# A third raw buffer and a second DMA queue for the second expert table of a decoder step on one Trainium2 core

## The reference, cut to what matters

```python
def one_block(xb):                 # 128 tokens at a time
    ...                            # scores of product keys, top 16 of 8 heads: eidx, gate
    u = u_tab[eidx]
    act = gelu(einsum('thkd,td->thk', u, xb))
    return einsum('thk,thkd->td', gate * act, v_tab[eidx])
out = x + peer; y = rmsnorm(out, w_norm_final)
```

## Time and profile before

| what | us |
|---|---|
| median of 3 runs (lowest, highest) | 3672.82 (3670.59, 3683.72) |
| the profiled execution's own time | 3685.51 |
| its span | 3683.6 |
| PE busy in the span | 3517.7 (95%) |
| DVE busy | 2571.1 (70%) |
| ACT busy | 1314.7 (36%) |
| POOL busy | 924.7 (25%) |

### The profile page before, as it was taken

How to read it: one execution, slowest core, us unless ns; L and a number is a source line. 1 busy time by engine, 2 the same in 40 slices (tenths; PEclk the granted TensorE clock), 3 DMA queues, 4 the chain that set the end, 5 groups by cost and what they waited for, 6 DMA issues and landing times. The chain is left out here.

```text
span 3683.6 us, 46625 instructions
## 1 busy us (share of the span) xinstructions
PE 3517.7 (95%) x17879; PEld 3071.5 (83%) x17879; DVE 2571.1 (70%) x3799; ACT 1314.7 (36%) x1675; POOL 924.7 (25%) x619
## 2 busy tenths in 40 slices
PE   8999999998989999999999999998999999999997
PEld 6877777776867889999999999997778787787885
DVE  4135545553233249999998888885888898898897
ACT  5111134442233223332237667762222232232223
POOL 0000000000000000233333333331444454454453
PEclk9999999999989999999999999999999999999998
DMA  5145343435334244788789999998889899899996
GB/s 204 48 147 168 112 135 128 144 110 184 139 122 146 86 176 152 274 320 340 294 323 360 381 384 379 380 384 338 349 334 363 337 347 364 338 348 363 356 356 264
DMA packets 193646, 964.86 MB, mean 262 GB/s; under 512 B 19697, under 2 KB 67121, under 8 KB 92706
## 3 DMA queue, kind: packets, MB, share of 16 engines
q1 hardware_dynamic: 121010, 516.50, 38.1%
q0 software_dynamic: 61424, 426.27, 29.8%
q10 hardware_dynamic: 11008, 19.26, 1.5%
HBM read 865.58 MB, written 96.37 MB: 261 GB/s over the span
## 5 line engine op out<-in xcount | busy, mean ns | idle before, releaser
L2068 PE MATMUL hidden_hp<-dense_hi,whi 128*128 128x384 f32 x2048 | 699.0, 341 | 6.1 <-PEq L123 6.1
L1836 ACT CAST whi<-raw 128x2048 fp32r<-128x2048 f32 x214 | 410.7, 1919 | 818.1 <-PE outputs_vp L2623 512.7
L2069 PE MATMUL hidden_hp<-dense_lo,whi 128*128 128x384 f32 x2048 | 690.8, 337 | 0.0
L2621 PE MATMUL outputs_vp<-whi,outputs_w_hi 128*128 128x512 f32 x1536 | 606.6, 395 | 51.4 <-DVE wlo L1840 38.3
L2015 POOL DMA_INDIRECT hidden_row<-u_rows,expert_ids x192 | 366.0, 1906 | 999.8 <-DVE dots L2300 621.9
L2622 PE MATMUL outputs_vp<-whi,outputs_w_lo 128*128 128x512 f32 x1536 | 603.8, 393 | 0.0
L2623 PE MATMUL outputs_vp<-wlo,outputs_w_hi 128*128 128x512 f32 x1536 | 603.1, 393 | 0.0
L1840 DVE TENSOR_TENSOR wlo<-raw,whi 128x2048 fp32r<-128x2048 f32 x214 | 490.0, 2290 | 111.0 <-ACT whi L1836 107.2
L2355 POOL DMA_INDIRECT outputs_row<-v_rows,outputs_id x192 | 373.0, 1943 | 561.0 <-DVE accg L2547 522.2
L2547 DVE SCALAR_TENSOR_TENSOR accg<-outputs_row,outputs_w_op,accg 128x2048 f32<-128x2048 f32 x192 | 451.3, 2351 | 88.5 <-DMA outputs_row<-v_rows,outputs_id 76.6
L2300 DVE CUSTOM_DVE_ANT_0 hidden_row<-hidden_row,hidden_h_row 128x2048 f32<-128x2048 f32 x192 | 436.8, 2292 | 66.9 <-DMA hidden_row<-u_rows,expert_ids 65.9
(11 more groups left out here) (384 smaller groups left out, 4901.0 us busy)
## 6 DMA issues: line engine op xcount, KB each, us to landing
raw<-v_units SPq DMA_DIRECT2D x128, 1024.0 KB
raw<-u_units SPq DMA_DIRECT2D x86, 1024.0 KB
raw<-w_in SPq DMA_DIRECT2D x42, 1024.0 KB, 5.5
hidden_raw<-u_units SPq DMA_DIRECT2D x42, 1024.0 KB
hidden<-hidden_hid SPq DMA_DIRECT2D x128, 192.0 KB
gate_mat<-units_big SPq DMA_DIRECT2D x12, 2048.0 KB, 20.2
units_big<-hidden SPq DMA_DIRECT2D x16, 1536.0 KB, 13.2
units_big<-gate_mat SPq DMA_DIRECT2D x16, 1536.0 KB, 18.9
```

Of the source, the lines that this page charges most:

```text
L1836: self.nc.scalar.copy(self.hi[s][:], self.raw[raw][:]).then_inc(self.hi_done, 1)
L2068: mm(o, un.hi[s][:, x, :], h_hi[:, x, :], start=x == 0, stop=False)
L2069: mm(o, un.hi[s][:, x, :], h_lo[:, x, :], start=False, stop=False)
L2621: mm(o[:], W_hi[s][:, e, at], hi[x][:, k, :], start=e == 0, stop=False)
```

## The change

Five edits, all for the stage `outputs`:

1. A third raw buffer (`deepen`), so the load of unit n+3 waits for the low part of unit n. SP then issues only the loads of the units.
2. The five loads of `sums` (the residual, 4.5 MB) at the stage's start go from SP's queue to ACT's, and SP's first DMA is the load of unit 2. Their semaphore is split in three, for the prompt rows, the sample rows and the dense tiles.
3. The two halves of a chunk's weights are issued by ACT, the hidden activations after the split of unit 0, the gates after that of unit 1. The DVE and ACT work on them moves one unit later: `weigh` to units 3 to 6, `weights_hi` to 5 and 7. `weights_lo` stays.
4. PE does a unit's 24 products with the high part first, after a wait for `hi_done`, and its 12 products with the low part after a wait for `lo_done`.
5. The loops of SP, ACT and DVE are written out (POOL keeps its loop).

```diff
+    def deepen(self, a):
+        self.raw[2], self.raw_in[2], self.deep = a.sb("raw2", [P, KT, P]), a.sem("raw_in2"), True
     def slot(self, n, s):
-        return n % U_RAW if isinstance(n, int) and n < NKEYS else s
+        if n < NKEYS:
+            return n % U_RAW
+        return (n - NKEYS) % U_RAW if self.deep else s
     def load(self, eng, n, s, table, at):
-        wait(eng, self.lo_done, n + 1 - U_RAW if isinstance(n, int) and n < NKEYS else n - 1)
+        wait(eng, self.lo_done, n + 1 - U_RAW if n < NKEYS or self.deep else n - 1)
...
         def _(sp):
-            def load_w(c):
-                wait(sp, w_lo_done, 2 * c)
-                load_chunk(sp, big, w_in, hidden, G, c)
-            def body(i):
-                for s in range(2):
-                    for j in range(DS):
-                        n = unit(i, s, j)
-                        if not (is_last(i, s) and j >= DS - 2):
-                            un.load(sp, NKEYS + n + 2, j % 2, v_units, n + 2)
-                        if j == 0 and not is_last(i, s):
-                            load_w(2 * i + s + 1)
-            ...                                       # five loads of sums
-            turns(sp, body, T)
+            un.load(sp, NKEYS + 2, 0, v_units, 2)
+            for n in range(DS * NCH - 3):
+                un.load(sp, NKEYS + n + 3, 0, v_units, n + 3)
...
         def _(act):
+            def load_w(c, x):
+                act.wait_ge(w_lo_done, 2 * c)
+                src = (hidden[c].rearrange("p a t -> p (a t)"), G[c].rearrange("p g a t -> p (g a t)"))[x]
+                act.dma_start(big[x][:, 0:CH * ND], src).then_inc(w_in, 16)
...
                             un.split_hi(act, NKEYS + unit(i, s, j) + 1, (j + 1) % 2)
-                        if j in (4, 6) and not is_last(i, s):
-                            weights_hi(2 * i + s + 1, 1 - s, (j - 4) // 2)
+                        if j < 2 and not is_last(i, s):
+                            load_w(2 * i + s + 1, j)
+                        if j in (5, 7) and not is_last(i, s):
+                            weights_hi(2 * i + s + 1, 1 - s, (j - 5) // 2)
...
+            act.dma_start(accg[0][:], sums[0:P, :]).then_inc(first_in, 16)
+            act.dma_start(accg[1][0:NSMP, :], sums[SEQ:SEQ + NSMP, :]).then_inc(sample_in, 16)
+            for t in range(DTILES):
+                act.dma_start(acc[t][:], sums[(t + 1) * P:(t + 2) * P, :]).then_inc(sums_in, 16)
...
         def _(vec):
-                        if 2 <= j < 6 and not is_last(i, s):
-                            weigh(c + 1, 2 * j - 4)
-                            weigh(c + 1, 2 * j - 3)
+                        if 3 <= j < 7 and not is_last(i, s):
+                            weigh(c + 1, 2 * j - 6)
+                            weigh(c + 1, 2 * j - 5)
...
         def _(pe):
-                    un.ready(pe, NKEYS + n)
+                    un.high(pe, NKEYS + n)
                     for t in range(DTILES):
                         if h == 0:
                             wait(pe, added, DTILES * (QB * c + q - 2) + t + 1)
...
                             mm(o[:], W_hi[s][:, e, at], hi[x][:, k, :], start=e == 0, stop=False)
                             mm(o[:], W_lo[s][:, e, at], hi[x][:, k, :], start=False, stop=False)
+                    un.ready(pe, NKEYS + n)
+                    for t in range(DTILES):
+                        o, at = vp[DTILES * (q % 2) + t], slice(t * P, (t + 1) * P)
+                        for k in range(HC):
+                            e = HC * h + k
                             ins = mm(o[:], W_hi[s][:, e, at], lo[x][:, k, :], start=False, stop=e == CH - 1)
                         ins.then_inc(un.done, 1)
```

More of the change, by code:

```diff
@@ L1820, in slot, with filled @@
     def slot(self, n, s):
-        return n % U_RAW if isinstance(n, int) and n < NKEYS else s
+        if n < NKEYS:
+            return n % U_RAW
+        return (n - NKEYS) % U_RAW if self.deep else s
+    def filled(self, n):
+        if n < NKEYS:
+            return 16 * (n // U_RAW + 1)
+        s, m = n % 2, n - NKEYS
+        if self.deep:
+            s, m = m % U_RAW, m // U_RAW
+        else:
+            m = m // 2
+        return 16 * (m + 1 + (len(range(s, NKEYS, U_RAW)) if s < 2 else 0))
     def load(self, eng, n, s, table, at):
-        wait(eng, self.lo_done, n + 1 - U_RAW if isinstance(n, int) and n < NKEYS else n - 1)
+        wait(eng, self.lo_done, n + 1 - U_RAW if n < NKEYS or self.deep else n - 1)
         s = self.slot(n, s)
@@ L1832, in split_hi @@
         raw = self.slot(n, s)
-        act.wait_ge(self.raw_in[raw], filled(n, s))
+        act.wait_ge(self.raw_in[raw], self.filled(n))
         wait(act, self.done, self.all_done(n - self.first - 1))
@@ L1849, in high @@
         pe.wait_ge(self.hi_done, n + 1)
[L1852 to L1856, removed]
 def turns(eng, body, count):
@@ L2386, in outputs @@
         lo = [x.rearrange("p k n -> p (k n)").rearrange("p (e d) -> p e d", d=NB) for x in un.lo]
-        added, weighed, gated, w_hi_done, w_lo_done, w_set, sums_in, cleared = (
-            a.sem(x) for x in ("added", "weighed", "gated", "w_hi_done", "w_lo_done", "w_set", "sums_in", "cleared"))
+        added, weighed, gated, w_hi_done, w_lo_done, w_set, cleared = (
+            a.sem(x) for x in ("added", "weighed", "gated", "w_hi_done", "w_lo_done", "w_set", "cleared"))
+        sums_in, first_in, sample_in = (a.sem(x) for x in ("sums_in", "first_in", "sample_in"))
         norm_in, squared, parts_done, moved, summed, meaned, rooted, done, stored, dstep = (
@@ L2400, in is_last @@
         def is_last(i, s):
-            return isinstance(i, int) and 2 * i + s == NCH - 1
+            return 2 * i + s == NCH - 1
         def rows_of(i, s, j):
@@ L2482, in roots @@
                 nc.scalar.activation(root[0:rows, at], mean[0:rows, at], ACT.Sqrt).then_inc(rooted, 1)
+            act.dma_start(accg[0][:], sums[0:P, :]).then_inc(first_in, 16)
+            act.dma_start(accg[1][0:NSMP, :], sums[SEQ:SEQ + NSMP, :]).then_inc(sample_in, 16)
+            for t in range(DTILES):
+                act.dma_start(acc[t][:], sums[(t + 1) * P:(t + 2) * P, :]).then_inc(sums_in, 16)
             weights_hi(0, 0, 0)
             weights_hi(0, 0, 1)
-            turns(act, body, T)
+            for i in range(T):
+                body(i)
             act.wait_ge(w_lo_done, 2 * NCH)
@@ L2542, in gathered @@
                 o = accg[j % 3 // 2]
-                if isinstance(i, int) and i == j == 0:
-                    vec.wait_ge(sums_in, 16 * TILES)
-                if isinstance(i, int) and i == 0 and j == 2:
+                if i == j == 0:
+                    vec.wait_ge(first_in, 16)
+                if i == 0 and j == 2:
+                    vec.wait_ge(sample_in, 16)
                     vec.wait_ge(cleared, 1)
@@ L2569, in body @@
                         if j > 0 and j % 2 == 0:
-                            add(c, j // 2 - 1, isinstance(i, int) and i == s == 0)
-                        if j == 0 and not (isinstance(i, int) and i == s == 0):
-                            add(c - 1, QB - 1, isinstance(i, int) and i == 0 and s == 1)
-                        if 2 <= j < 6 and not is_last(i, s):
-                            weigh(c + 1, 2 * j - 4)
-                            weigh(c + 1, 2 * j - 3)
+                            add(c, j // 2 - 1, c == 0)
+                        if j == 0 and c > 0:
+                            add(c - 1, QB - 1, c == 1)
+                        if 3 <= j < 7 and not is_last(i, s):
+                            weigh(c + 1, 2 * j - 6)
+                            weigh(c + 1, 2 * j - 5)
                         if j in (5, 7) and not is_last(i, s):
@@ L2585, in _ @@
                 weights_lo(0, 0, x)
-            turns(vec, body, T)
+            for i in range(T):
+                body(i)
             vec.wait_ge(squared, 1)
```

9 lines of the change are left out of this document (3 added, 6 removed).

## The result

| | before | after |
|---|---|---|
| median of 17 runs each (lowest, highest), us | 3676.64 (3666.3, 3690.92) | 3686.96 (3684.08, 3693.94) |
| profiled execution's own time, us | 3685.51 | 3693.94 |

The ratio is 1.0033, with a 95% interval of [1.0023, 1.0043]: the change makes the kernel 0.33% slower, 12 us. 3637 us was forecast, with a range up to 3672, which does not hold it. One execution each of two kernels further down, w_on_sp and written_out, took over 12 ms: their medians count it in, their ratios leave it out.

A forecast was written before the change was run, and what follows sets the result against it. PE was busy 95%, so only its waits and slow matmuls could be won: 47.4 - 3 - 2 = 42.4 us off the profiled 3685.51 gives 3643. The middle of 3643 and 3630 was taken: 3637 us, range 3615 to 3672.

The forecast's parts named there:

- Third buffer: In the last stage, unit loads issued a unit earlier remove 12 PE waits after 2600 and slow matmuls: 47.4 us won.
- what is late next?: After raw loads, DVE if anything: 7 us a chunk left against 4.8 of row waits; 3 us kept for PE waits.
- The other queue: In the last stage, 35 more DMA issues on ACT, which sat idle before its casts: cost 0, bounds 0 and 18 us.
- rival (b): In the last stage, the third queue starves the gathers while weights load, so it gets slower: 3700 us, chance 0.07.
- Weights' work a unit later: In each chunk, ACT has `weights_hi` done by the time DVE needs it: cost 0.
- Low parts last: In each PE unit, high-part products first: valued at 0 by itself, bounds 0 and 12 x 2.3 = 28 us.
- written out: Register instructions of the loops on DVE, ACT and SP go: 0, bounds 3 us won and 5 lost.
- loads of `sums` on ACT's queue: At the stage's start, `sums` is in 37 us later, at 2582; priced within the start's 2 us loss.
- The start: At the stage's start, a new PE wait of 7 to 13 us against earlier waits gone: 2 us lost.
- The end: After the last matmul, DVE's last add stays behind the rows' norm: 0, bounds 0 and 5 us lost.
- What would show it: Signs in the last stage: ACT's `raw` idle below 60 us, near 365 GB/s, units 8.16 us apart, gathers landing in 11 to 13.

The follow-up runs named there:

- w_on_sp: The changed kernel, but with a chunk's weights issued whole on SP's queue again: 3662.95 us, 0.9949 of the kernel before.
- written_out: The kernel before with its loops on SP, ACT and DVE written out, nothing else: 3688.99 us, ratio 1.0008.
- third_only: The kernel before with the third raw buffer and its programs written out, nothing else: 3645.04 us, 0.9904 of the kernel before.
- combo_row_moved: third_only with low parts last, `sums` loaded on ACT's queue and one gathered row moved from a chunk's unit 1 to unit 2: 3633.21 us, 0.9881 of before.
- third_w_on_act: third_only with the weights in halves on ACT's queue and the work on them a unit later: 3695.83 us, 1.0044 of the kernel before.
- third_halves_on_sp: third_weigh_late with the weights' halves issued by SP in units 0 and 1: 3649.37 us, 0.9921 of the kernel before.
- third_w_on_act_early: third_only with both halves of the weights issued by ACT in unit 0 instead of SP: 3704.98 us, 1.0068 of the kernel before.
- third_weigh_late: third_only with DVE's and ACT's work on the next chunk's weights a unit later: 3665.74 us, 0.9957 of the kernel before.

## Why the prediction was wrong

- **Third buffer, 47.4 us less 3 for what stays.** Right in itself: third_only gains 35 to 44 us, its ten PE waits sum to 11.4 us, of which 5.2 lie at the start. The change does take the waits on raw buffers away. What failed is "what is late next?", in the sum the 3 us for PE waits that remain: after unit 5 PE waits 36.3 us in 14 places, and units are 0.45 us longer than 8.16 on average, 55 us over 122 units. So 36.3 us are waits and the other 18.6 slow matmuls behind them, 1.3 for each as worked out (a mean: in the kernel before, the granted clock was 0.50 from 2726.2 to 2729, behind a wait of 3.94 us, and 1.00 from 2656.7 to 2660, behind one of 2.24). I set DVE's waits, 4.8 us a chunk, against 7 us of slack a chunk and called it close. With the change they are 136.8 / 16 = 8.6 us a chunk, and they don't spread over the chunk: 123 us of them lie in two units, ahead of a low part. DVE can make low parts at most one unit ahead of PE (there are two `wlo` buffers), so the slack of the other six units is of little use. combo_row_moved bears this out, with 85.7 us of row waits and 0.7 us of PE's on a low part. Before the change, too, the row waits lay in these two units.
- **The other queue, cost 0.** This is the step that failed most: I priced ACT's issues by the instructions (0 to 18 us) and left the bytes to rival (b). Measured with nothing else changed: 45 us (third_w_on_act against third_halves_on_sp) and 60 us (third_w_on_act_early against third_only). Together with the cut in halves, which by itself wins, it is 31 us (after against w_on_sp) and 32 us (third_w_on_act against third_weigh_late).
- **Rival (b), chance 0.07.** It is what happened, with the mechanism as written: the gathers' part falls from nearly a half to about a third. My reason against it, that three row buffers would be full when the weights start, is false: two are being used up at that moment, as the timeline shows. Its price, +27 us for the whole change, was too high: it took the loss at half of its worst case (which would be 30) from the time before, while the runs show 45 to 60 us for the queue and 35 to 44 of gain from the third buffer beside it, +12 in all. My threshold of 10 us of row waits a chunk was too high, by the same mistake with means: 8.6 was enough.
- **Weights' work a unit later, cost 0.** Wrong, 19 us. I looked at whether DVE would have ACT's result in time, not at the gather that is issued near the weights: with the later work it comes behind them instead of ahead. Why, stays open.
- **Low parts last, 0; written out, 0; loads of `sums` on ACT's queue.** Right: 1 us; 1.0008 with an interval of [0.9987, 1.0029], which holds 1; 2 us.
- **The start, a PE wait of 7 to 13 us and a 2 us loss.** The mechanism was right and the times near: DVE waits 10.02 us for the gates at 2599.76 and its low part starts at 2605.42; 2601 and 2606.7 were worked out. But PE's wait is 5.34 us, below the range, and the start is a gain: unit 5 ends at 2610.5, before at 2588.91 + 3 x 8.16 = 2613.4.

```profile
2599.76 1.03 DVE L2524 TENSOR_TENSOR units_big<-units_big 128x384 f32<-128x384 f32 x2 [10.02 <-DMA units_big<-gate_mat]
2600.70 4.80 DVE L2556 SCALAR_TENSOR_TENSOR accg<-outputs_row,outputs_w_op,accg 128x2048 f32<-128x2048 f32 x2
2605.42 2.28 DVE L1857 TENSOR_TENSOR wlo<-outputs_raw,whi 128x2048 fp32r<-128x2048 f32 x1
```

- **The end, 0, bound 5.** 4.4 us lost: the last row is done later, the norm behind it too, and the last add begins 8.2 us after the last matmul instead of 4.0.

```profile
3655.75 2.35 DVE L2556 SCALAR_TENSOR_TENSOR accg<-outputs_row,outputs_w_op,accg 128x2048 f32<-128x2048 f32 x1
...
3669.18 1.87 DVE L2544 TENSOR_TENSOR acc<-acc,outputs_vp 128x512 f32<-128x512 f32 x3
```

- **What would show it.** ACT's idle on `raw` fell below 60 (to 0), gathers land 11.4 us after their issue (11 to 13 said). But the stage ran at 350 GB/s, not 365, and the units after the start are (3660.9 - 2610.5) / 122 = 8.61 us apart (2610.5 is the end of unit 5, whose low part PE starts at 2607.76), over the 8.4 at which I called the forecast wrong.

## What to carry to other kernels

Before a bulk transfer goes to a queue of its own, ask which other queue lives on its share: a queue more takes from all that have work, and the one whose data is wanted soonest pays. Judge slack over the stretch in which the waits fall and by how far the waiting engine can run ahead, not by means over a longer period. And where a late transfer can't be avoided, look at what stands between it and the critical engine in program order: here one row moved by one unit was worth 7 to 11 us.

## What the runs showed of the hardware

The rate of the DMA engines did not depend on the number of queues (2.52 to 2.55 MB in 6 us with two and with three), but their division did. While all three had work, packets went out in equal numbers (91, 93 and 92), and the weights' packets are the larger ones (1.07 MB in 91, 11.8 KB, against 0.74 MB in 92, 8.0 KB, for the gathers), so the bulk queue took more bytes and more time (41.7% against 29.0%) than the queue that was in a hurry. The issue of a gather on POOL lasted 0.96 us at one place and 4.85 us at another of the same chunk of third_only (2929.53 and 2935.12).
